# First norm per token tile, selected scores between the transposes, sample transposes ahead of weighted sums

## What is computed

```python
def rms_norm(x, g):
    xf = x.astype(jnp.float32)
    y = xf * lax.rsqrt(jnp.mean(xf * xf, axis=-1, keepdims=True) + RMS_EPS)
    return (y * g.astype(jnp.float32)).astype(x.dtype)
...
h = rms_norm(x, P['norm_mix'][l])
z = jnp.einsum('btd,de->bte', h, P['w_in_even'][li])
...
# for each query and head: three branches, each with its own softmax
o = g[..., 0:1] * o_c + g[..., 1:2] * o_s + g[..., 2:3] * o_w
```

## Time and profile before

| | us |
|---|---|
| median of 3 runs (lowest, highest) | 1857.3 (1855.72, 1863.38) |
| the profiled execution: its own time | 1855.83 |
| its span in the trace | 1854.0 |
| PE busy | 1757.1 (95%) |
| DVE busy | 816.4 (44%) |
| ACT busy | 528.7 (29%) |
| POOL busy | 703.4 (38%) |

### The profile page before, as it was taken

One profiled execution on the slowest core, in us unless ns is written; L12 is line 12 of the kernel. 1 busy time (PEld: TensorE's weight loads), 2 busy tenths in 40 slices (PEclk: granted clock), 3 DMA queues, 4 the chain that ended last, 5 costly groups with the idle time before them and its releaser, 6 DMA issues.

```text
span 1854.0 us, 35860 instructions
## 1 busy us (share of the span) xinstructions
PE 1757.1 (95%) x15660; PEld 1672.2 (90%) x15660; DVE 816.4 (44%) x1645; ACT 528.7 (29%) x908; POOL 703.4 (38%) x282
## 2 busy tenths in 40 slices
PE   6989888889979998999999999999999999999998
PEld 5977777579857996999999999999999999999998
DVE  4261686323473444554530445443245555014531
ACT  5232555323331222332211222322223222112221
POOL 1200000013214011656644555656565655446642
PEclk8988799999979997999999999999999999999999
DMA  5540520522101000222222221332222222222222
GB/s 146 122 63 23 167 81 13 159 84 74 47 10 48 4 4 27 87 74 77 77 85 81 91 88 49 103 103 70 92 78 82 72 89 74 86 92 81 71 72 92
DMA packets 159419, 140.83 MB, mean 76 GB/s; under 512 B 16186, under 2 KB 154974, under 8 KB 158878
## 3 DMA queue, kind: packets, MB, share of 16 engines
q1 hardware_dynamic: 159262, 138.53, 25.3%
HBM read 132.62 MB, written 10.02 MB: 77 GB/s over the span
## 4 chain that ended last, share of the span: by engine, by line
PE 69%; DVE 1%; POOL 0%; ACT 0%; issue 0%
PE ps L310 60%; PE ps L2163 8%; PE ps L2626 0%; PE ps L2352 0%; PE ps L2605 0%; PE ps L2611 0%; PE ps L494 0%; PE ps L2423 0%; PE ps L543 0%; DVE y_gated L2876 0%; DVE mixf L2878 0%; DVE mix_lo L2872 0%; PE ps L491 0%; POOL mix_lo L2668 0%; PE ps L492 0%
## 5 line engine op out<-in xcount | busy, mean ns | idle before, releaser
L271 POOL TENSOR_TENSOR w_lo<-w_raw,w_hi 128x2048 fp32r<-128x2048 f32 (+3 forms) x109 | 459.3, 4214 | 781.4 <-ACT w_hi L265 781.2
L310 PE MATMUL ps<-h_hi,w_hi 128*128 128x288 f32 x1792 | 385.0, 296 | 0.0
L310 PE MATMUL ps<-h_hi,w_lo 128*128 128x288 f32 x1792 | 384.4, 295 | 0.0
L310 PE MATMUL ps<-h_lo,w_hi 128*128 128x288 f32 x1792 | 384.3, 295 | 0.0
L265 ACT ACTIVATE w_hi<-w_raw 128x2048 fp32r<-128x2048 f32 (+3 forms) x109 | 190.0, 1743 | 482.9 <-PE ps L310 442.1
L310 PEld LDWEIGHTS ps<-h_hi,w_hi 128*128 128x128 f32 x1792 | 287.2, 188 | 0.3
L310 PEld LDWEIGHTS ps<-h_hi,w_lo 128*128 128x128 f32 x1792 | 286.9, 188 | 0.0
L310 PEld LDWEIGHTS ps<-h_lo,w_hi 128*128 128x128 f32 x1792 | 286.9, 188 | 0.0
L310 PE MATMUL ps<-g_hi,w_hi 128*128 128x288 f32 x704 | 151.6, 296 | 0.0
L310 PE MATMUL ps<-g_hi,w_lo 128*128 128x288 f32 x704 | 151.0, 295 | 0.0
L310 PE MATMUL ps<-g_lo,w_hi 128*128 128x288 f32 x704 | 151.0, 295 | 0.0
(11 more groups left out here) (502 smaller groups left out, 3002.0 us busy)
## 6 DMA issues: line engine op xcount, KB each, us to landing
w_raw<-in_ffn_up SPq DMA_DIRECT2D x44, 1024.0 KB, 5.1
w_raw<-in_ffn_down SPq DMA_DIRECT2D x16, 768.0 KB, 4.6
w_raw<-in_w_in_odd SPq DMA_DIRECT2D x12, 1024.0 KB, 5.2
w_raw<-in_ffn_down SPq DMA_DIRECT2D x16, 640.0 KB, 4.3
w_raw<-in_w_in_even SPq DMA_DIRECT2D x7, 1024.0 KB, 5.3
w_raw<-in_w_in_even SPq DMA_DIRECT2D x6, 872.0 KB, 10.1
BT<-rv SPq DMA_DIRECT2D x8, 520.0 KB, 3.9
seg<-in_cache_cmp_kv SPq DMA_DIRECT2D x32, 128.0 KB
```

The costliest lines, as they stand in the source:

```text
L271: pool.tensor_tensor(slab_view(wlo[slot], st), slab_view(raw[slot], st), slab_view(whi[slot], st).bitcast(F32), ALU.subtract).then_inc(w_l ...
L310: last = pe.matmul(ps[:, bank + 2 * j + half, 0:HT], w[slot][:, c:c + 128], x[:, xs + t, half * HT:(half + 1) * HT], start=(t == 0 and n = ...
```

## The change

1. **First norm per tile.** ACT takes a square root of a dummy column first, then works tile by tile: sum of squares, root of one column (the mean before and the reciprocal after it on DVE, put between DVE's copies), scaling. Slab 0 is split in two halves (`w0_hi`, `w0_lo`) after the second tile is scaled; `products_tok` waits for the second half only ahead of the fifth of eight weight tiles. Tile 4's squares come after the first two half tiles are rounded.
2. **Prompt attention.** Score jobs are split into "selected" and "others"; the exponentials run S, W, C instead of C, S, W, and the S one signals by itself (`ps_ready`). PE's list becomes the one in the diff: S transposes, selected scores of u + 2, W and C transposes, other scores, values S, W, C. ACT copies PTs before PTc.
3. **Sample attention.** `outputs_back` of the group before stands behind the eight transposes instead of ahead of them.

```diff
@@ products_tok
-                pe.wait_ge(w_lo_ready, g + 1)
+                if g >= 1:
+                    pe.wait_ge(w_lo_ready, g + 1)
...
                     for t in range(KT):
+                        if g == 0 and tok == 0 and t == 0:
+                            pe.wait_ge(w0_lo, 1)
+                        if g == 0 and tok == 0 and t == KT // 2:
+                            pe.wait_ge(w_lo_ready, 1)
@@ first block, ACT
                     act.wait_ge(cleared, 1)
-                    for t in range(5):
+                    act.activation(xsq[:, 0:1], xss[:, 0:1], ACT.Sqrt).then_inc(sqrt_table, 1)
+                    act.wait_ge(sqrt_table, 1)
...
-                    split_hi(act, *follow(0))
-                    act.wait_ge(ss_taken, 1)
-                    act.activation(xss[:, :], xss[:, :], ACT.Sqrt).then_inc(std_ready, 1)
+                    def root(t):
+                        act.wait_ge(ss_taken, t + 1)
+                        act.activation(xss[:, t:t + 1], xss[:, t:t + 1], ACT.Sqrt).then_inc(std_ready, 1)
...
+                    square(0)
+                    square(1)
+                    root(0)
+                    square(2)
+                    root(1)
                     scaled(0)
+                    square(3)
+                    root(2)
                     scaled(1)
-                    for n in range(10):
+                    act.wait_ge(w_loaded[0], 16)
+                    act.activation(whi[0][:, 0:HALF0], raw[0][:, 0:HALF0], ACT.Copy).then_inc(w0_hi, 1)
+                    act.activation(whi[0][:, HALF0:KT * NSA_W], raw[0][:, HALF0:KT * NSA_W], ACT.Copy).then_inc(w_hi_ready, 1)
+                    root(3)
+                    high(0)
+                    high(1)
+                    square(4)
+                    high(2)
+                    high(3)
+                    scaled(2)
+                    root(4)
+                    scaled(3)
+                    high(4)
+                    high(5)
+                    scaled(4)
+                    for n in range(6, 10):
                         high(n)
@@ first block, DVE: between the ten copies of xT
+                        if n in (2, 4, 6):
+                            mean_square(n // 2 - 1)
+                        if n in (3, 5, 8):
+                            inverse_root((3, 5, 8).index(n))
...
+                        if n == 2:
+                            inverse_root(3)
+                        if n == 4:
+                            mean_square(4)
+                        if n == 6:
+                            inverse_root(4)
@@ prompt attention, PE
-                        if u >= 1:
-                            pe.wait_ge(s_taken, u)
+                        if u >= 2:
+                            pe.wait_ge(s_taken, u - 1)
...
+                        pe.wait_ge(ps_ready, u + 1)
+                        if u >= 1:
+                            pe.wait_ge(pt_act, u)
+                        for kt in range(qt + 1):
+                            last = pe.transpose(ps[:, 5, 128 * kt:128 * kt + 128], sS[s][:, 128 * kt:128 * kt + 128], ident[:, :])
+                        last.then_inc(pts_ready, 1)
+                        if u + 2 < U:
+                            scores(u + 2, "selected")
                         pe.wait_ge(p_ready, u + 1)
                         if u >= 1:
-                            pe.wait_ge(pt_act, u)
                             pe.wait_ge(pt_dve, u)
                         for kt in range(qt + 1):
-                            pe.transpose(ps[:, 5, ...
                             pe.transpose(ps[:, 6, ...
                         if u + 2 <= U:
                             pe.wait_ge(s_taken, u + 2)
+                        if u >= 1:
+                            pe.wait_ge(ptc_act, u)
                         pe.transpose(ps[0:32, 4, 256:384], sC[s][:, :], ident[:, :]).then_inc(pt_ready, 1)
                         if u + 2 < U:
-                            scores(u + 2)
+                            scores(u + 2, "others")
                         pe.wait_ge(pt_act, u + 1)
-                        pe.wait_ge(pt_dve, u + 1)
                         if u >= 1:
                             pe.wait_ge(o_taken, u)
                         O = ps[:, 7, 0:192]
-                        pe.matmul(O[:, 0:64], PTc[:, :], ...
                         for n, (PT, c0) in enumerate(((PTs, 896), (PTw, 1152))):
+                            if n == 1:
+                                pe.wait_ge(pt_dve, u + 1)
...
+                        pe.wait_ge(ptc_act, u + 1)
+                        pe.matmul(O[:, 0:64], PTc[:, :], vc[0:32, 2, 64 * g:64 * g + 64], start=True, stop=True).then_inc(o_ready, 1)
@@ prompt attention, ACT
-                        (exponential of sC first, then sS, then sW -> p_ready)
+                        (exponential of sS -> ps_ready, then sW, then sC -> p_ready)
...
-                        act.wait_ge(pt_ready, u + 1)
+                        act.wait_ge(pts_ready, u + 1)
                         if u >= 1:
                             act.wait_ge(o_ready, u)
+                        act.copy(PTs ...).then_inc(pt_act, 1)
+                        act.wait_ge(pt_ready, u + 1)
                         act.copy(PTc ...).then_inc(ptc_act, 1)
-                        act.copy(PTs ...).then_inc(pt_act, 1)
@@ sample attention, PE
-                        if grp >= 1:
-                            outputs_back(grp - 1)
                         pe.wait_ge(sp_ready, grp + 1)
                         for br in range(2):
                             for kt in range(4):
                                 last = pe.transpose(ps[:, 5 + br, ...
                             last.then_inc(spl_ready, 1)
+                        if grp >= 1:
+                            outputs_back(grp - 1)
```

More of the change, by code:

```diff
@@ L1150, in _ @@
                 def _(pool):
-                    for g in range(6):
+                    for lo, hi, s_hi, s_lo in ((0, HALF0, w0_hi, w0_lo), (HALF0, KT * NSA_W, w_hi_ready, w_lo_ready)):
+                        pool.wait_ge(s_hi, 1)
+                        pool.tensor_tensor(wlo[0][:, lo:hi], raw[0][:, lo:hi], whi[0][:, lo:hi].bitcast(F32), ALU.subtract).then_inc(s_lo, 1)
+                    for g in range(1, 6):
                         split_lo(pool, *follow(g))
@@ L1228, in _, with mean_square, inverse_root @@
                         dve.nop().then_inc(s, 2)
+                    def mean_square(t):
+                        dve.wait_ge(ss_ready, t + 1)
+                        dve.tensor_scalar(xss[:, t:t + 1], xss[:, t:t + 1], 1.0 / D, EPS, ALU.mult, ALU.add).then_inc(ss_taken, 1)
+                    def inverse_root(t):
+                        dve.wait_ge(std_ready, t + 1)
+                        dve.reciprocal(xrs[:, t:t + 1], xss[:, t:t + 1]).then_inc(rs_ready, 1)
                     for n in range(10):
@@ L1622, in scores @@
                         for n, (out, keys) in enumerate(jobs):
+                            if (n == 0) != (branches == "selected"):
+                                continue
+                            if n == 2 and u >= 1:
+                                pe.wait_ge(s_taken, u)
                             if n == 2 and u >= 2:
@@ L1626, in scores @@
                             last = pe.matmul(out, q, keys[1], start=False, stop=True)
-                        last.then_inc(s_ready, 1)
-                    scores(0)
-                    scores(1)
+                        if branches != "selected":
+                            last.then_inc(s_ready, 1)
+                    for u in range(2):
+                        scores(u, "selected")
+                        scores(u, "others")
                     for u in range(U):
```

29 lines of the change are left out of this document (12 added, 17 removed).

## The result

The changed kernel takes 1836.4 us (median of 4 runs, 1833.18 to 1842.17), against 1856.9 us for the kernel before beside it (4 runs): ratio 0.9886, 95% interval 0.9864 to 0.9909. The profiled execution took 1833.18 us, with a span of 1831.3 us.

A forecast was written before the change was run, and what follows sets the result against it. TensorE, busy 95% of the span, was taken as the bound. Terms -6.0 - 0.6 - 1.9 + 1.0 - 1.9 = -9.4 us against 1855.8 gave 1846.4, or 1847.9 against the median; stated 1847.5, range 1840.5 to 1855.

The forecast's parts named there:

- Prompt attention at 0.50: Attention block's opening stretch at half clock: PE is never idle there, so the new order gains 0.
- clock stretches of the remaining stages: Unchanged stages move with their start; their lower-clock stretches may fall otherwise, 2 to 3 us either way.
- The ring: Prompt attention at full clock, DVE-PE loop of onat, copy and values: about 0.85 us less per four-unit cycle, -6.0 us.
- the last unit: End of prompt attention, no scores behind it: values start once the C transpose and unit 30's onat finish, -0.6 us.
- Rival B: Prompt attention: PTw comes late and DVE has no room, so attention gives only 2 us; 1852.8 us total, chance 0.23.
- D: First block: alternating roots and squares on ACT would reload tables each time; no time of its own, no separate chance.
- The first norm: First block: PE starts the projection at 19.05 for 24.03, but the block's end moves only -1.9 us.
- the cap: First block: slab 3 arrives only 1.9 us earlier, not 5, leaving PE idle some 3 us ahead of g = 3.
- rival A: Program start: slab 3 lands 5 us sooner, the full 5 us is kept, no clock fall; 1843.5 us, chance 0.18.
- the charge of +1.0 for a clock fall: First block: PE's new idle time may lower the clock; half such a fall charged, +1.0 us, bounds 0 and +2.5.
- The sample part: Sample attention: groups 1, 2 and 3 change by -1.6, +0.7 and -1.0 us, together -1.9 us.
- Rival C: Attention block: more PE waits keep the clock at 0.50, +2.5 us a unit; near 1868 us with eight units, chance 0.04.

## Why the prediction was wrong

**Where it failed.** "*Prompt attention at 0.50.* ... Reordering a full engine gives nothing: 0", and that the clock stretches of the remaining stages "can fall otherwise by a stretch or so, 2 to 3 us either way". Its first part holds for an order at a given clock, but it took the length of the stretch at 0.50 as given. The 31 executions with the whole new attention order (the change, the attention part alone, the changes without the sample part and with slab 3 early) have a median of 1836.2 us and spend 111.4 us at 0.50, against 136.4 before: 25 us less. At 0.38 us each that is 9.5 of the 21.8 us between the medians. The parts alone say which edit does it: 109 us at 0.50 with the attention part, 130 with the first norm, 131 with the sample part, 134 in the kernel before beside them. Within it, the selected scores ahead of the window transposes hold 14 of the 25 us. Why that order keeps the clock up isn't settled: with them behind, the cycle is the same and the clock is not. That PE's idle time ahead of the block matters is shown, since filling it gave the old order as large a relief.

**The ring** (-6.0, and -0.6 for the last unit) was right: 2.98 and 3.73 us for "2.9 to 3.0" and "3.7 to 3.8", 12.98 a cycle, and 6.3 to 6.4 us at equal clock for 6.6. Two steps of the walk were off: it laid the gain on values that no longer wait for PTw, and that gives only qt = 2, while qt = 3 needs the S transposes signalled apart as well; and it charged the selected scores 0.26 to 0.55 us a unit for a late PTw, where they cost the cycle nothing. The DVE waits came as foretold (9.6 to 3.4, new ones ahead of PTw). Rival B (2 us) fell. So did D: the first block has one table load, 1.28 us at 0.74, and its roots and squares then alternate without another.

**The first norm** was too small. PE starts at 20.20 for the 19.05 walked, because the two `h_lo` steps beside POOL's halves take 1.21 and 1.85 us and not 0.68. But the cap behind it hardly binds: slab 3 came 3.2 us sooner and not 1.9, and the wait ahead of g = 3 is 0.75 us for "2 to 4". The compression block begins at 114.0 to 115.8 us in the eleven profiles with this part (median 115.0) and at 116.8 to 123.9 in the seven without (median 118.3): -3.3 for -1.9, between the forecast and rival A's 5. Part of it is the clock: those with the part have at most 6.8 us at 0.50 in the first block, five of the seven without have 10.2 or 13.7. The two without that have 6.8 begin at 116.83 and 118.05, 1.8 and 3.0 us behind 115.0. The spread of those without it comes from slab 3 too, for which PE waited up to 4.2 us in them. That a low part is "just in time already" was one execution's luck. Nor did the charge of +1.0 for a clock fall come: the fall moved from PE's old idle time into the new one, and the first block's time at 0.50 was 6.8 us here and 13.7, 10.2 or 6.8 before.

**The sample part** (-1.9) was right only where GpSimd doesn't interfere. With the stall gone from both kernels, the interval behind group 1 shrinks from 15.56 to 14.97 us (the former in the old order with filler, whose maximum took 0.16 us; the kernel before with GpSimd late has 17.15 there, with 3.4 us of it at 0.50), that behind group 2 from 15.57 to 14.99, and from group 3's exponentials to the block's end it is 15.94 for 16.90: -0.6, -0.6 and -1.0 for the -1.6, +0.7 and -1.0 forecast, together -2.2. Two whole sample blocks without a stall, the old order with filler and the fourth profile of the whole change, agree (72.21 and 70.13 us, with 3.4 and 4.1 us at 0.50):
```profile
328.59:400.80 72.21, 57.61 (x368) 37.87 (x369) 22.46 (x98) 23.36 (x61) 4.52 (x1) 0.98 0.38 113
```
```profile
308.21:378.34 70.13, 58.14 (x368) 37.88 (x369) 22.48 (x98) 23.04 (x61) 4.52 (x1) 0.97 0.38 117
```
The kernel before with GpSimd late has 73.99, with 7.7 us at 0.50. With the stall, as in three of four profiles of the whole change, the second term turns into a loss: 17.71 and 14.66 us behind groups 1 and 2, where the second profile of before has 18.48 and 13.03. That leaves -0.6 to nothing (blocks of 73.5 to 73.6 us for 73.5 and 74.1 before), which the part's own run can't tell from nothing. The prediction took from one profile that in group 2 "`acc` and the exponentials end together, the transposes at 370.20 cannot start sooner", and did not ask why those exponentials came late: the held maximum.

**The sum.** At equal clock: attention -6.3 to -6.4, start -1.8 to -3.0, sample from nothing to -2.2, so -8 to -12 for the forecast -9.4. The fitted line of the 31 executions has the slope of that of the 68, 0.38, and lies 12 us under it, at the upper end of that. So the forecast's own sum held about as well as these runs can tell, and the clock's 9.5 us, which it had at nothing, carried the time out of its range. **Rival C** had the right mechanism with the wrong sign. The clock did decide, and the prediction's fault was to price it at 0.04 for slower and at "a little for avoided clock stretches" for faster (0.05 of chance, and nothing in the sum), with a stretch of 22 us at half speed in its rows. The rule of the Trainium skill that it cited (TensorE: Matmul & The Clock Gate, section "A second HAM failure mode: psum-queue depth-cycling") tells of a kernel with matmuls of 512 columns in bf16 in which short idle times between groups of matmuls make the clock swing. On one trace the prediction found no swing in this loop; the filler runs have falls at 216 us, in the midst of it, and at 290, near its end. So the clock does fall and rise within the loop, as by that rule. That the short idle times are the reason no run here shows.

## What to carry to other kernels

Where a stage of small matmuls shows 0.50 in one profile although PE is busy, the length of that stretch is a term of the sum with both signs: read the clock of every execution, not of the profiled one alone, and compare kernels at equal clock before a gain is put down to a schedule. Reordering short matmuls in such a stage was worth more here through the clock (9.5 us) than in the cycle (6.4), and the place of the selected scores only through the clock. And where a small VectorE operation takes microseconds, look at what GpSimd ran until its end. In a ring over engines, shortening one link shows only in the units whose next-longest link allows it, so walk each shape of unit on its own.

## What the runs showed of the hardware

The same program spends between 122 and 160 us at 0.50 from one execution to the next (68 executions of the kernel before), which is worth some 14 of its 1858 us. 5.9 us of transposes that compute nothing took 27 us off the average of the 19 executions beside them.

VectorE operations on SBUF were held or slowed while GpSimd ran a subtraction of its own. The 128x2 maximum took 2.75 to 3.55 us for 0.16 in twelve profiles and ended within 0.03 us of GpSimd's subtraction each time; in the first block `h_lo` (128x512) took 1.21 and 1.85 us for 0.68, while `hf` beside it, which reads PSUM, took its usual 0.67. The Trainium skill (GPSIMD Engine Reference, section "1. Specifications") says that GpSimd shares its SBUF interfaces with VectorE and contends with its instructions that have two SBUF inputs or run in a 2-port mode. By that rule `mx` and `h_lo` should suffer and `hf` should not, and the trace agrees. An operation with one tensor input was held as well: a multiplication of `rs` (128x40) by a constant, at 88.17 us in the changed kernel, took 3.75 us and ended 0.03 us after GpSimd's subtraction; another operation of its shape, beside which GpSimd stood idle, took 0.18 us.
